# First attention's scores as three rounded products instead of one full fp32 product, with a new order inside a step and smaller rings

## The reference

```python
h = rms_norm(x, mix_norm_g[0])
proj = h @ a_w_in[0]                      # q, k, v for 16 heads of 64, and 16 gates
c = cumsum(log_sigmoid(gates + a_b_f))    # per head
for i in range(4):                        # query blocks of 128
    s = q[q0:q1] @ k[:q1].T * 64 ** -0.5 + c[q0:q1, None] - c[None, :q1]
    p = softmax(where(causal, s, -inf))
    out = p @ v[:q1]
x = x + out @ a_w_out[0]
```

## Time and profile before

| what | value |
|---|---|
| runs | 2595.57 us median of 3 |
| the profiled execution | 2596.87 us, span 2595.0 us, granted clock 0.999 |
| TensorE busy | 2577.5 us, 99% |
| VectorE / ScalarE busy | 1389.8 us (54%) / 979.9 us (38%) |
| stage `ain` with steps 0 to 20 | about 64 to 197.5 us of the span |
| steps 21 to 25 | 197.5 to 217.6 us |

### The profile page before, as it was taken

One profiled execution on the slowest core, in us unless ns is written; L12 is line 12 of the kernel. 1 busy time (PEld: TensorE's weight loads), 2 busy tenths in 40 slices (PEclk: granted clock), 3 DMA queues, 4 the chain that ended last, 5 costly groups with the idle time before them and its releaser, 6 DMA issues.

```text
span 2595.0 us, 30845 instructions
## 1 busy us (share of the span) xinstructions
PE 2577.5 (99%) x12344; PEld 2110.2 (81%) x12344; DVE 1389.8 (54%) x2182; ACT 979.9 (38%) x1537; POOL 135.1 (5%) x178
## 2 busy tenths in 40 slices
PE   9999999999999999999999999999999999999999
PEld 7777888888889788888866888888888888888887
DVE  5555773664434776376586544344553466543343
ACT  5454442343225644244446432233223433332231
POOL 1310000000001100000020000000111300000000
PEclk9999999999999999999999999999999999999999
DMA  4321322232232123223230223223232122233232
GB/s 166 101 74 66 98 89 99 97 107 98 96 106 66 42 98 105 98 90 106 96 97 33 97 98 98 89 98 105 90 114 65 57 97 92 96 97 106 97 98 82
DMA packets 67200, 240.30 MB, mean 93 GB/s; under 512 B 8016, under 2 KB 8144, under 8 KB 66928
## 3 DMA queue, kind: packets, MB, share of 16 engines
q1 hardware_dynamic: 63504, 227.81, 26.5%
q0 software_dynamic: 3552, 10.51, 1.3%
HBM read 235.56 MB, written 2.13 MB: 92 GB/s over the span
## 4 chain that ended last, share of the span: by engine, by line
PE 95%; DVE 2%; ACT 2%; issue 1%; DMA 0%; SPq 0%; POOL 0%; DVEq 0%; ACTq 0%
PE ps L469 30%; PE ps L471 29%; PE ps L470 29%; PE ps L582 1%; PE ps L942 1%; PE ps L597 1%; PE ps L617 1%; ACT m_B_P L1933 1%; PE ps L920 1%; ACT m_E_P L1933 0%; PE ps L534 0%; DVE m_E_P L1110 0%; DMA m_x<-in_xT 0%; PE ps L797 0%; DVE m_wsp L991 0%
## 5 line engine op out<-in xcount | busy, mean ns | idle before, releaser
L469 PE MATMUL ps<-m_xs,m_wsp 128*128 128x512 f32 x2152 | 845.3, 393 | 0.3 <-DVE m_wsp L991 0.3
L471 PE MATMUL ps<-m_xs,m_wsp 128*128 128x512 f32 x2152 | 838.3, 390 | 0.0
L470 PE MATMUL ps<-m_xs,m_wsp 128*128 128x512 f32 x2152 | 837.9, 389 | 0.0
L1824 ACT ACTIVATE m_wsp<-m_raw 128x1024 fp32r<-128x1024 f32 (+1 forms) x426 | 442.8, 1051 | 723.4 <-PE ps L471 693.4
L991 DVE TENSOR_TENSOR m_wsp<-m_raw,m_wsp 128x1024 fp32r<-128x1024 f32 (+1 forms) x426 | 511.4, 1217 | 103.4 <-ACT m_wsp L1824 103.1
L469 PEld LDWEIGHTS ps<-m_xs,m_wsp 128*128 128x128 f32 x2152 | 404.4, 188 | 93.7 <-issue 10.2
L471 PEld LDWEIGHTS ps<-m_xs,m_wsp 128*128 128x128 f32 x2152 | 404.2, 188 | 84.6
L470 PEld LDWEIGHTS ps<-m_xs,m_wsp 128*128 128x128 f32 x2152 | 404.4, 188 | 84.1 <-issue 1.4
L1044 DVE TENSOR_TENSOR m_x<-m_x,ps 128x512 f32<-128x512 f32 x104 | 71.0, 687 | 315.0 <-PE ps L471 315.0
L469 PE MATMUL ps<-m_wsp,m_xs 128*128 128x512 f32 x320 | 127.9, 400 | 3.7 <-DVE m_xs L1018 3.2
L471 PE MATMUL ps<-m_wsp,m_xs 128*128 128x512 f32 x320 | 125.8, 393 | 0.0
(11 more groups left out here) (345 smaller groups left out, 3308.9 us busy)
## 6 DMA issues: line engine op xcount, KB each, us to landing
m_raw<-in_w SPq DMA_DIRECT2D x424, 512.0 KB, 3.3
m_A_cb<-csum POOLq DMA_DIRECT2D x16, 256.0 KB, 3.7
m_x<-in_xT SPq DMA_DIRECT2D x4, 512.0 KB, 8.4
m_B_bias<-in_biasB POOLq DMA_DIRECT2D x8, 256.0 KB, 3.5
out<-m_x SPq DMA_DIRECT2D x8, 256.0 KB, 2.4
m_raw<-in_w SPq DMA_DIRECT2D x4, 256.0 KB, 6.7
m_O_D<-in_decay POOLq DMA_DIRECT2D x1, 1024.0 KB, 5.8
m_E_q<-m_sq POOLq DMA_DIRECT2D x16, 32.0 KB, 1.9
```

The lines of the kernel that those rows point to most:

```text
L469: e.matmul(out, lh, rh, start=first, stop=False)
L470: e.matmul(out, lh, rl, start=False, stop=False)
L471: return e.matmul(out, ll, rh, start=False, stop=final)
L1824: e.activation(wsp[n % NSP][:, 0, o:1024], raw[n % NRAW][:, o:1024], ACT.Copy).then_inc(*s_hi(n))
```

## The change

Queries and keys are stored as two fp32r parts. VectorE scales a group from PSUM into `sqs[0]` (q) or `sqs[1]` (k); ScalarE rounds that into part 0 of `A_q` or `A_k`; VectorE subtracts to make part 1 (`ain_low`), in the next chunk, behind that chunk's `lo`. `A_q` and `A_k` become rings of two pairs. The scores are three fp32r products for every old fp32 matmul, still on 64 rows and with the two heads in turn. Scores come first in a step of A. Steps stand after tiles 6, 10 and 15. `A_cb` has 4 buffers instead of 6, `A_P` 7 instead of 8.

```diff
-A_SPOTS = [(4, 0, 1), (9, 1, 1), (14, 2, 1)]
+A_SPOTS = [(6, 0, 1), (10, 1, 1), (15, 2, 1)]
...
-            A_q = sb(c, "A_q", [128, 8, S])
-            A_k = sb(c, "A_k", [128, 8, S])
+            A_q = ring(c, "A_q", 2, [128, 2, S], F32R)
+            A_k = ring(c, "A_k", 2, [128, 2, S], F32R)
...
-            A_cb = ring(c, "A_cb", 6, [128, 7 * 128])
-            A_P = ring(c, "A_P", 8, [128, S])
+            A_cb = ring(c, "A_cb", 4, [128, 7 * 128])
+            A_P = ring(c, "A_P", 7, [128, S])
...
+                            if pre == "A":
+                                for qi, ki in ((0, 0), (0, 1), (1, 0)):
+                                    for j, (o, n, keys) in zip(u.jobs, part):
+                                        s = j.segs[si]
+                                        last[j] = e.matmul(bank(pre, "score", j.n)[:, s["c0"] + o:s["c0"] + o + n],
+                                                           spec["q"](u, j, s)[:, qi, :], keys[:, ki, :],
+                                                           start=(qi, ki) == (0, 0), stop=qi == 1)
+                                continue
...
                 def step(i):
+                    if pre == "A" and i < n:
+                        scores(units[i])
                     if lag <= i < n + lag:
                         turn(units[i - lag])
-                    if EARLY[pre] <= i < n:
+                    if pre != "A" and EARLY[pre] <= i < n:
                         scores(units[i])
...
-            project(ST["ain"], xhalf, lambda k: s_xlo["mix0", k], lambda m: s_ev["ain", m],
+            project(ST["ain"], xhalf, lambda k: s_xlo["mix0", k], lambda m: s_step["ain", m],
...
                     q.wait_ge(*s_mm["ain", m])
                     q.wait_ge(*s_rowc["mix0"])
+                    if m % 8:
+                        q.wait_ge(*s_ev["ain", m - 1])
+                    t = sqs[m // 8]
...
+            def ain_low(m):
+                to = (A_k if m >= 8 else A_q)[m % 8 % 2]
+                q.wait_ge(*s_aev["ain", m])
+                e.tensor_tensor(to[:, 1, :], sqs[m // 8][:, :], to[:, 0, :].bitcast(F32), ALU.subtract).then_inc(*s_ev(("ain", m)))
...
+                    if c:
+                        ain_low(ST["ain"].groups[c - 1][0])
+                    if c in steps_at:
+                        loop(*steps_at[c])
...
+            ain_low(15)
             loop(21)
...
+            def ain(g):
+                m = g[0]
+                p = m % 8
+                q.wait_ge(*s_step["ain", m])
+                if p >= 2:
+                    q.wait_ge(*s_score["A", A_units[3 * (p - 2) + 2].jobs[-1].n])
+                e.activation((A_k if m >= 8 else A_q)[p % 2][:, 0, :], sqs[m // 8][:, :], ACT.Copy).then_inc(*s_aev(("ain", m)))
```

More of the change, by code:

```diff
@@ L283, in build @@
             A_o = sb(c, "A_o", [128, 2, 8, S], F32R)
-        with ExitStack() as c:
-            A_q = sb(c, "A_q", [128, 8, S])
-            A_k = sb(c, "A_k", [128, 8, S])
+            A_q = ring(c, "A_q", 2, [128, 2, S], F32R)
+            A_k = ring(c, "A_k", 2, [128, 2, S], F32R)
             A_v = sb(c, "A_v", [128, 4, 1024])
@@ L290, in build @@
                 A_onr = sb(c2, "A_onr", [16, S])
-            A_cb = ring(c, "A_cb", 6, [128, 7 * 128])
-            A_P = ring(c, "A_P", 8, [128, S])
+                A_wf = sb(c2, "A_wf", [128, 8, 16])
+            A_cb = ring(c, "A_cb", 4, [128, 7 * 128])
+            A_P = ring(c, "A_P", 7, [128, S])
             A_PT = ring(c, "A_PT", 4, [128, S])
             A_st = ring(c, "A_st", 8, [128, 16])
-            A_wf = sb(c, "A_wf", [128, 8, 16])
         F_act, F_u, F_t, F_v = [], [], [], []
@@ L371, in E_factor @@
             return E_nrm[:, i, :].rearrange("p (t j r) -> p t j r", t=4, j=4)[:, tb:tb + n, h % 4, h // 4]
-        first_squares = A_P[0:7]
+        first_squares = A_P
         A_units, B_units, E_units = causal_units(8, ((0,), (1, 0), (2, 0, 1), (0, 1, 2, 3))), dilated_units(), causal_units(4)
@@ L671, in A_keys @@
             def A_keys(u, j, s):
-                k = A_k[64 * j.par:64 * j.par + 64, u.p, :]
+                k = A_k[u.p % 2][64 * j.par:64 * j.par + 64, :, :]
                 qb = s["qb"]
                 if qb in (0, 3):
-                    return [(0, s["n"], k[:, 0:s["n"]])]
-                return [(0, 128, k[:, 128 * qb:128 * qb + 128]), (128, 128 * qb, k[:, 0:128 * qb])]
+                    return [(0, s["n"], k[:, :, 0:s["n"]])]
+                return [(0, 128, k[:, :, 128 * qb:128 * qb + 128]), (128, 128 * qb, k[:, :, 0:128 * qb])]
             scores, step = attention("A", A_units, dict(
                 P=A_P, PT=A_PT, among=nothing, to=in_order, ready=A_ready, vready=[s_aev["av", 1, 2], s_ev["av", 3]],
-                q=lambda u, j, s: A_q[64 * j.par:64 * j.par + 64, u.p, 128 * s["qb"]:128 * s["qb"] + 128],
+                q=lambda u, j, s: A_q[u.p % 2][64 * j.par:64 * j.par + 64, :, 128 * s["qb"]:128 * s["qb"] + 128],
                 k=A_keys,
@@ L1251, in ain @@
                     q.wait_ge(*s_rowc["mix0"])
+                    if m % 8:
+                        q.wait_ge(*s_ev["ain", m - 1])
+                    t = sqs[m // 8]
                     if m < 8:
-                        i = e.scalar_tensor_tensor(out=A_q[:, m, :], in0=bank("ain", m)[:, :], scalar=0.125,
+                        i = e.scalar_tensor_tensor(out=t[:, :], in0=bank("ain", m)[:, :], scalar=0.125,
                                                    in1=rb("mix0")[:, :], op0=ALU.mult, op1=ALU.mult)
                     else:
-                        i = e.tensor_tensor(A_k[:, m - 8, :], bank("ain", m)[:, :], rb("mix0")[:, :], ALU.mult)
-                    i.then_inc(*s_ev(("ain", m)))
+                        i = e.tensor_tensor(t[:, :], bank("ain", m)[:, :], rb("mix0")[:, :], ALU.mult)
+                    i.then_inc(*s_step(("ain", m)))
+            def ain_low(m):
+                to = (A_k if m >= 8 else A_q)[m % 8 % 2]
+                q.wait_ge(*s_aev["ain", m])
+                e.tensor_tensor(to[:, 1, :], sqs[m // 8][:, :], to[:, 0, :].bitcast(F32), ALU.subtract).then_inc(*s_ev(("ain", m)))
             def A_bias(u, j, s):
-                cb = A_cb[j.h % 6]
+                cb = A_cb[j.h % 4]
                 if s["qb"] == 1:
@@ L1267, in vector_program, with among_tiles, hook @@
             over(ST["av"], rows_out(ST["av"], A_v, rc("mix0"), s_col["mix0"]), {5: [forget], 6: [forget_sum]})
-            over(ST["ain"], ain, {c: [lambda a=a, b=b: loop(a, b)] for c, a, b in A_STEPS})
+            steps_at = {c: (a, b) for c, a, b in A_STEPS}
+            def among_tiles(c):
+                def hook():
+                    if c:
+                        ain_low(ST["ain"].groups[c - 1][0])
+                    if c in steps_at:
+                        loop(*steps_at[c])
+                return hook
+            over(ST["ain"], ain, {c: [among_tiles(c)] for c in range(16)})
+            ain_low(15)
             loop(21)
@@ L2035, in scalar_program @@
                  {6: [forget]})
-            over(ST["ain"], nothing, {c: [lambda a=a, b=b: loop(a, b)] for c, a, b in A_STEPS})
+            def ain(g):
[5 more added lines that the diff above has]
+                e.activation((A_k if m >= 8 else A_q)[p % 2][:, 0, :], sqs[m // 8][:, :], ACT.Copy).then_inc(*s_aev(("ain", m)))
+            over(ST["ain"], ain, {c: [lambda a=a, b=b: loop(a, b)] for c, a, b in A_STEPS})
             loop(21)
@@ L2359, in A_sums @@
             def A_sums(h):
-                if h >= 6:
-                    q.wait_ge(*s_top["A", A_units[3 * ((h - 6) // 2) + 2].jobs[-1].n])
-                load(A_cb[h % 6][:, 384:896], a["csum"][h:h + 1, :].broadcast_to([128, S]), d_cb[h % 6], ("cb", h))
+                if h >= 4:
+                    q.wait_ge(*s_top["A", A_units[3 * ((h - 4) // 2) + 2].jobs[-1].n])
+                load(A_cb[h % 4][:, 384:896], a["csum"][h:h + 1, :].broadcast_to([128, S]), d_cb[h % 4], ("cb", h))
             def A_masked(h):
-                cb = A_cb[h % 6]
+                cb = A_cb[h % 4]
                 q.wait_ge(*d_mk["mk"])
-                q.wait_ge(*d_cb[h % 6]["cb", h])
+                q.wait_ge(*d_cb[h % 4]["cb", h])
                 three, one = (mask[:, :].rearrange("p (b n) -> p b n", b=1).broadcast_to([128, 3, 128]), mask[:, :])
@@ L2371, in A_masked @@
                 e.tensor_tensor(cb[:, 768:896], cb[:, 768:896], one, ALU.add).then_inc(*s_masked(h))
-            for hs in (range(6), *(range(h, h + 2) for h in range(6, 16, 2))):
+            for hs in (range(4), *(range(h, h + 2) for h in range(4, 16, 2))):
                 for h in hs:
```

## The result

| | before | after |
|---|---|---|
| median | 2595.72 us (6 runs, 2593.63 to 2598.10) | 2605.47 us (6 runs, 2602.19 to 2606.16) |
| profiled execution | 2596.87 us, span 2595.0 | 2602.19 us, span 2600.4 |

The ratio is 1.0032, 95% interval 1.0022 to 1.0042: slower by 8.3 us, between 5.7 and 10.9. The two medians of six are 9.8 us apart. Forecast were +7.4 us, 2603, range 2597 to 2612. The profiled execution of the changed kernel is the fastest of its six, 3.3 us under their median; what follows is read from it.

What follows compares the result with a forecast made beforehand. TensorE, busy 99% of the span, was taken as the bound. Products 1.5, order 3.0, end 2.1 and clock 0.8 sum to +7.4 us, with inside cover and rings at 0: 2603 us predicted, range 2597 to 2612.

Steps and rivals of the forecast that it cites:

- The products, +1.5: Scores in `ain`: three fp32r products per old fp32 matmul cost +0.19 us a pair of heads, +1.5 for 8.
- no overlap: Rival, scores: the two half-row heads don't overlap in fp32r; 2612 us, or 2622 in full; chance 12%.
- by columns: Rival, scores: narrow product pairs take time by their columns (0.06 us for 128); 2598 us; chance 8%.
- The order in a step, +3.0: Steps 4 to 23 of `ain`: transposes behind 64-row scores pay one more border, 0.15 us each, +3.0 us.
- borders between fp32r shapes are free: Rival, TensorE's steps in `ain`: changing shape between two fp32r groups costs nothing; 2597.6 us; chance 9%.
- The way to the scores, 0 inside: PSUM to scores inside `ain`: three instructions in a row are covered by later tiles, 1.3 us to spare; cost 0.
- 7 times: Inside `ain`: the 1.3 us of cover ahead of the scores was claimed to hold seven times, at cost 0.
- The end, +2.1: End of `ain`: TensorE starts step 21's scores 1.42 us later with 0.66 of transposes still to do, +2.1 us.
- The clock, +0.8: End of `ain`: an idle piece of about 2.4 us may lower TensorE's clock, +1.7 us or 0; half put in.

Runs made afterwards that it cites:

- The old order: Changed kernel with transposes, scores, `weighted` in each step, as before the change, instead of scores first: median 2600.44 us, ratio 1.0018.
- One fp32 product: Changed kernel with one fp32 matmul of the high parts in place of the three fp32r products: one run, 2603.33 us.
- the fp32 kernel: Kernel before with one edit, scores first in a step of A, still fp32 with its own spots and rings: 2600.25 us, ratio 1.0015.
- the old spots: Changed kernel with its steps back after tiles 4, 9 and 14: median 2604.74 us, ratio 1.0037.
- TensorE kept at work: Changed kernel with 11 unused fp32 products of ones ahead of step 21, during the wait for the last keys: 2601.40 us, ratio 1.0024.
- the second profile: Profile of the changed kernel run again, unchanged: profiled execution 2605.46 us; median of that repeat 2604.55 us, ratio 1.0035.
- a filled end: Step 21 as transposes, `weighted`, scores in the changed kernel: 2600.82 us, 1.0018; with transposes before scores in all other steps too, 2598.83 us, 1.0010.

## Why the prediction was right

- *The products, +1.5.* The old order left 1.06 in seven pairs, so 0.15 a pair and +1.2. The direction was right and the pace too, each unit within 0.06: 1.15 for the 1.21 forecast, 0.89 for 0.89, 0.90 for 0.88. By the starts of single records a narrow pair goes at 0.112, as taken, a pair of 256 columns at 0.118, as taken, and one of 512 at 0.235 for the 0.227. The 0.06 too much is in the rest: the first unit has 1.15 - 9 x 0.112 = 0.14, where 0.20 was forecast; the second has its 0.20. That the pace was hit to the nanosecond is partly luck: the forecast's rows gave only a mean of 0.117 for both narrow widths on 128 rows, and how it was split was a choice. The rivals "no overlap" and "by columns" fell with these pieces; that the load is what paces is still argued. The Trainium skill, "TensorE: Matmul & The Clock Gate", section "LDWEIGHTS (loading the stationary operand)", has a load take its columns divided by 1.2 GHz, 107 ns for 128, whatever its rows. The 0.112 between narrow pairs is 5 ns over it; the load records themselves last 188 ns and overlap.
- *The order in a step, +3.0.* 0.15 at each of the transposes, as read in the earlier trace rows from another pair of shapes; 2.37 to 2.58 in the 17 steps inside the stage, in both types. With the 0.45 of the last three steps that is +2.8 to +3.0. The rival "borders between fp32r shapes are free" fell: the first product behind a group is 0.43 as before, and the scores' pieces still have 0.14 to 0.20 beyond their pace. One fp32 product kept the new border, and the fp32 kernel got it. The Trainium skill, "TensorEngine Tiling (Array Packing)", under Key Properties, says that a change of tiling mode drains TensorE; the 0.15 at each new border agrees.
- *The way to the scores, 0 inside.* In the profile after, the subtraction for k3 ends at 142.30 and the first score record is at 143.86, 1.56 us later, for the 1.3 us forecast, which had no handover in it; less the 0.26 of the handover 1.3 are left. It holds so in the last five pairs inside the stage. In the one for k1 the distance is only 0.38 (85.41 to 85.79), so "7 times" came within 0.1 us of being wrong there. With the old spots the cover fails by 0.9 us in all, so it was real and needed.
- *The end, +2.1.* The end went from 12.33 to 14.73 without the clock (TensorE kept at work), +2.40. Of this 3 borders are 0.45 and one pair's products 0.15, which are counted above, so +1.8. The way there was only half right. I had the wait (the last product starts at 198.72 and has 0.23, the scores start at 201.59, 2.64 later; forecast 2.46), but counted 0.66 of the cost as TensorE's transposes that stand behind it. With these brought forward, at a clock that stays up, the end is only 0.6 shorter (14.12 for 14.73), and with the old order everywhere it still is 2.17 above before: the rest is a later start of ScalarE's chain.
- *The clock, +0.8.* This term was mis-sized, and is the one that was furthest off. I gave a fall of the clock an even chance and 3.4 us of it; at this place it came in seven profiles of seven. It cost 1.4 us where it lasted 3.4 (16.12 - 14.73) and 2.8 where it lasted 6.8 (17.56 - 14.73). The 1.7 forecast for 3.4 us was 0.3 too much, and that it can last longer was not foreseen.
- *Sum.* 1.2 + 3.0 + 1.8 + 1.4 = +7.4 for the first profile, whose two distances give +7.2; with the 2.8 of the second it is +8.8, whose distances give +8.7. The measured +8.3 holds all of them in its interval. That the first sum is the forecast's 7.4 to the tenth is luck: products and end were 0.3 each too high, the clock 0.6 too low.

**Open.** The two medians are 9.8 and 8.9 above before. The profiled runs are accounted for: the second profile's 2605.46 is 8.6 above the 2596.87 of before, its two distances give +8.7, and each of the two has 3.4 us of lower clock twice elsewhere. The first profile's 2602.19 is 5.3 above, for +7.2 less the 2.0 ahead of the stage. The medians are not accounted for: how long the lower clock lasted in the other runs isn't known, as they have no profile. The profiles show the lower clock at three other places too (about 10, 880 and 1397 us): none, one or two of them in a profile, and in kernels of both kinds. Whether the change makes those likelier isn't settled; nothing was run for it.

No version with the change beat the kernel before. The nearest, with the old order and a filled end, is 3.0 us slower: 1.06 in the stage and 2.17 at its end, of which the new spots are some 0.4 by the kernel before with the new spots. The old order with the old spots and a filled end was not run.

## What to carry to other kernels

Before fp32 matmuls are split in three rounded products, look at their width. A pair of products of 128 columns whose weights are used once was paced here at 0.112 us, and one of 256 at 0.118, so at these widths the cost of three products doesn't follow their columns. Here, for a pair of heads on the two halves of the rows and without the border, three take 0.34 us at 128 columns where the full fp32 matmul takes 0.22, 0.35 for 0.44 at 256, and 0.70 for 0.86 at 512.

Read the pieces of the chain for what a group costs over its count times its pace. That rest came with each change of the array's shape here and was paid at each border, so the order of the groups has a price of its own.

An idle piece on a full TensorE can cost more than its length. Behind pieces of 2.1 to 2.5 us the clock fell in every profile here, and that cost 1.4 to 2.8 us more; useless matmuls in the piece saved it. When such a piece is removed, ask what waits next: here a good part of it came back as waits for ScalarE.

When versions are compared by one profile each, put the stretches at the lower clock beside them. Two profiles of the same changed kernel differ by 3.3 us by these alone.

## What I had not expected

- Filling 2.5 us of idle time with products of ones took 3.2 us off the median (2604.55 to 2601.40). In the profiles of the two kernels that ran beside each other 2.8 of it is at the end of the stage (17.56 and 14.73), all by the clock.
- The three products of one head, put before those of the other, still ran in twos 10 ns apart, at 1.16 us for 1.15.
- The lower clock behind the idle piece lasted 3.4, 6.8 or 10.2 us in different profiles.
